# A hybrid decoder step on one core: the sample stage's first keys, last page and gate weights in another order

## What is computed

```python
def diff_attention(q, k, v, q_pos, k_pos, lam, lambda_init, subln):
    s = jnp.einsum("bqhmd,bkhmd->bhmqk", q, k) * (DH_D ** -0.5)
    s = jnp.where(k_pos[None, :] <= q_pos[:, None], s, -jnp.inf)
    p = jax.nn.softmax(s, axis=-1)
    a = p[:, :, 0] - lam * p[:, :, 1]
    o = jnp.einsum("bhqk,bkhv->bqhv", a, v)
    return rmsnorm(o, subln) * (1.0 - lambda_init)

# sample side: keys and values of the cache pages, then the own ones
k_all = jnp.concatenate([past_k, kd], axis=1)
v_all = jnp.concatenate([past_v, vd], axis=1)
o = diff_attention(qd, k_all, v_all, pos, k_pos, lam, lambda_init, subln)
...
y_b = o.reshape(B, T, D_D) @ w_proj_b
merged = jax.nn.sigmoid(g_a) * y_a + jax.nn.sigmoid(g_b) * y_b
x = x + merged @ w_out
x = x + 0.5 * swiglu(rmsnorm(x, ffn2_norm), ffn2_w_gate, ffn2_w_up, ffn2_w_down)
```

## Time and profile before

| | us |
|---|---|
| time, median of 3 runs (lowest to highest) | 1717.48 (1714.74 to 1723.19) |
| the profiled execution: time | 1720.7 |
| the profiled execution: span, first to last instruction | 1718.9 |
| PE busy in the span | 1664.8 (97%) |
| DVE, ACT busy | 765.6, 554.3 |

### The profile page before, as it was taken

How to read it: one execution, slowest core, us unless ns; L and a number is a source line. 1 busy time by engine, 2 the same in 40 slices (tenths; PEclk the granted TensorE clock), 3 DMA queues, 4 the chain that set the end, 5 groups by cost and what they waited for, 6 DMA issues and landing times.

```text
span 1718.9 us, 30602 instructions
## 1 busy us (share of the span) xinstructions
PE 1664.8 (97%) x12820; PEld 1571.5 (91%) x12820; DVE 765.6 (45%) x1150; ACT 554.3 (32%) x845; POOL 4.3 (0%) x20
## 2 busy tenths in 40 slices
PE   7999999999999999999999999989999999999996
PEld 7999999999988666999999977669999999999996
DVE  3333333333682433453336678664454333333332
ACT  5222222222332433442211257562234222222222
POOL 0000000000000000000000000000000000000000
PEclk8999999999999999999999999999999999999998
DMA  4322223322322740233333340553322332223231
GB/s 117 98 85 85 85 85 87 98 84 75 77 74 55 249 144 0 64 89 91 91 96 96 78 182 26 186 159 87 93 86 79 91 90 86 85 85 102 85 85 53
DMA packets 253837, 161.77 MB, mean 94 GB/s; under 512 B 8235, under 2 KB 246048, under 8 KB 253763
## 3 DMA queue, kind: packets, MB, share of 16 engines
q1 hardware_dynamic: 253616, 160.67, 32.2%
q10 hardware_dynamic: 146, 0.04, 0.0%
HBM read 143.14 MB, written 16.40 MB: 93 GB/s over the span
## 4 chain that ended last, share of the span: by engine, by line
PE 88%; ACT 3%; DVE 3%; DMA 2%; issue 1%; SPq 1%; ACTq 0%; DVEq 0%
PE ps L402 72%; PE ps L781 2%; PE ps L969 2%; PE ps L933 1%; PE ps L1257 1%; PE ps L1128 1%; PE ps L1185 1%; DMA Cb<-in_state_C 1%; PE ps L1018 1%; PE ps L1301 1%; PE ps L1113 1%; DVE small L2327 1%; PE ps L1182 1%; PE ps L1260 1%; DMA vecs<-in_subln 0%
## 5 line engine op out<-in xcount | busy, mean ns | idle before, releaser
L402 PE MATMUL ps<-xn_hi,w_hi 128*128 128x272 f32 (+1 forms) x2192 | 634.9, 290 | 4.7 <-DVE w_lo L374 2.6
L402 PE MATMUL ps<-xn_hi,w_lo 128*128 128x272 f32 (+1 forms) x2192 | 636.8, 290 | 0.0
L402 PE MATMUL ps<-xn_lo,w_hi 128*128 128x272 f32 (+1 forms) x2192 | 633.8, 289 | 0.0
L370 ACT ACTIVATE w_hi<-raw 128x1024 fp32r<-128x1024 f32 (+1 forms) x200 | 222.1, 1111 | 822.8 <-PE ps L402 818.2
L402 PEld LDWEIGHTS ps<-xn_hi,w_hi 128*128 128x128 f32 x2192 | 413.0, 188 | 6.3 <-DVE w_lo L374 3.1
L402 PEld LDWEIGHTS ps<-xn_hi,w_lo 128*128 128x128 f32 x2192 | 412.7, 188 | 0.0
L402 PEld LDWEIGHTS ps<-xn_lo,w_hi 128*128 128x128 f32 x2192 | 411.8, 188 | 0.0
L374 DVE TENSOR_TENSOR w_lo<-raw,w_hi 128x1024 fp32r<-128x1024 f32 (+1 forms) x200 | 257.5, 1288 | 214.8 <-ACT w_hi L370 214.2
L402 PE MATMUL ps<-h_lo,w_hi 128*128 128x280 f32 (+1 forms) x704 | 204.7, 291 | 0.0
L402 PE MATMUL ps<-h_hi,w_hi 128*128 128x280 f32 (+1 forms) x704 | 204.7, 291 | 0.0
L402 PE MATMUL ps<-h_hi,w_lo 128*128 128x280 f32 (+1 forms) x704 | 204.6, 291 | 0.0
(11 more groups left out here) (372 smaller groups left out, 2043.6 us busy)
## 6 DMA issues: line engine op xcount, KB each, us to landing
raw<-in_w_in SPq DMA_DIRECT2D x56, 512.0 KB, 3.9
raw<-in_ffn_w_gate SPq DMA_DIRECT2D x44, 512.0 KB, 3.8
raw<-in_ffn_w_up SPq DMA_DIRECT2D x44, 512.0 KB, 3.8
raw<-in_ffn_w_down SPq DMA_DIRECT2D x32, 704.0 KB, 4.5
Cb<-in_state_C SPq DMA_DIRECT2D x32, 256.0 KB, 4.0
out<-Cb SPq DMA_DIRECT2D x32, 256.0 KB, 3.1
pages<-in_cache_k SPq DMA_DIRECT2D x16, 512.0 KB, 4.5
pages<-in_cache_v SPq DMA_DIRECT2D x16, 512.0 KB, 4.7
```

The costliest lines, as they stand in the source:

```text
L370: act.activation(w_hi[s][:, 0:p.nk, :], raw[s][:, 0:p.nk, :], ACT.Copy).then_inc(hi_done[s], 1)
L402: mm = pe.matmul(ps[:, bank + half, 0:p.half], w[s][:, k, :], x[:, k0 + k, cols], start=first and k == 0 and a == 0, stop=last and k == p. ...
```

## The change

Six edits, all in and around the sample stage:

1. PE transposes the first three groups of the first page of keys in the last steps of "attend": behind `output(G - 3)`, ahead of `transposed(G - 1)` (G = 34 steps). They use banks that the scores had, after the last exponentials. The fourth group follows when PE's stage is over, and PE's `begin` is gone.
2. ACT and DVE copy the first keys ahead of their barrier. `head_square(0)`, `(1)` and DVE's `memset` of `AT3` come behind them. `head_sum(0)` moves from ahead of `score(0)` to behind it.
3. The last page of keys goes to slot 1 instead of slot 0.
4. SP loads the first gate panel to `raw[0]` when sequence 4's values are done, behind the last page in its queue; only the other panel waits for all keys.
5. ACT and DVE split that panel inside the loop at sequence 7: ACT ahead of the last exponentials, DVE ahead of the last mask and maximum.
6. PE runs four gate tiles ahead of `probabilities(7)`, two behind it, then `values(7)`, two and the second half's first, `back(1)`, three more, the sum, and the last four.

```diff
-        SLOTS = [i % 5 for i in range(13)] + [3, 4, 0]
+        SLOTS = [i % 5 for i in range(13)] + [3, 4, 1]
-        SUM_KEYS, SUM_SCORE = {0: 0, 1: 2, 2: 4, 3: 7}, {0: 1, 1: 3, 2: 5}
+        SUM_KEYS, SUM_SCORE = {1: 2, 2: 4, 3: 7}, {0: (0, 1), 1: (3,), 2: (5,)}
...
+            sp.wait_ge(sv_full, 5)
+            load(sp, p_b, 0, 0)
             sp.wait_ge(keys_full, 4 * NB)
-            stream_short(p_b)
+            load(sp, p_b, 0, 1)
+            for j in range(1, p_b.n):
+                load(sp, p_b, j, 0)
+                load(sp, p_b, j, 1)
...
                 if g >= 4:
                     output(g - 4)
+                if g == G + 1:
+                    pe.wait_ge(e_ready, G)
+                    keys(0, range(3))
             end(pe, pe_stage)
-            begin(pe, "sample")
...
             for b in range(NB):
-                keys(b)
+                keys(b, range(4) if b else range(3, 4))
...
-            probabilities(NB - 1)
             pe.wait_ge(evac[0], p_b.ev0)
             pe.wait_ge(lo_done[0], p_b.before + 1)
-            gate_part(0, range(2))
+            gate_part(0, range(4))
+            probabilities(NB - 1)
+            gate_part(0, range(4, 6))
             values(NB - 1)
-            gate_part(0, range(2, 5))
+            gate_part(0, range(6, DT))
+            gate_part(1, range(1))
             back(1)
-            gate_part(0, range(5, DT))
+            gate_part(1, range(1, 4))
             pe.wait_ge(osq_ready, HD + 1)
             pe.matmul(ps[:, 4, 0:HD * NS], ones[:, :], ofac[:, :, NP_:T], start=True, stop=True).then_inc(ring_full, 1)
-            gate_part(1, range(DT)).then_inc(mm_done[0], 1)
+            gate_part(1, range(4, DT)).then_inc(mm_done[0], 1)
...
-            begin(act, "sample")
+            act.wait_ge(tail_in, HD)
...
-            act.wait_ge(stored, 16 * (5 + 6))
-            head_square(0)
...
+                if b == 0:
+                    begin(act, "sample")
+                    act.wait_ge(stored, 16 * (5 + 6))
+                    head_square(0)
+                    head_square(1)
+                for h in (2,) if b == 0 else ():
+                    head_square(h)
+                if b == NB - 1:
+                    act.wait_ge(keys_full, 4 * NB)
+                    split_hi(act, p_b, 0, 0)
                 act.wait_ge(smax_ready, b + 1)
...
-            split_hi(act, p_b, 0, 0)
...
-            begin(v, "sample")
+            v.wait_ge(tail_in, HD)
+            for i in range(2):
+                v.tensor_copy(KT[0][i][:, :, PAST:PAST + NS], own_k[:, 4 * i:4 * i + 4, :])
...
+                if b == NB - 1:
+                    v.wait_ge(sv_full, NB - 2)
+                    split_lo(v, p_b, 0, 0)
                 v.wait_ge(ss_full, b + 1)
...
-            split_lo(v, p_b, 0, 0)
```

More of the change, by code:

```diff
@@ L1306, in output, with keys @@
                 mm.then_inc(o_full, 1)
+            def keys(b, groups=range(4)):
+                page_wait(pe, (0, b))
+                for n in range(4 * b + groups[0], 4 * b + groups[-1] + 1):
+                    g, q = n % 4 // 2, n % 2
+                    if n >= 3:
+                        m = n - 3
+                        if m % 2 == 0:
+                            pe.wait_ge(keys_act, m // 2 + 1)
+                        else:
+                            pe.wait_ge(keys_dve, m // 2 + 1)
+                    for i in range(4):
+                        hh = 4 * q + i
+                        mm = transpose(ps[:, n % 3, 128 * i:128 * i + 128],
+                                       pages[page_slot((0, b))][:, g, 128 * hh:128 * hh + 128], 128)
+                    mm.then_inc(keys_full, 1)
             for g in range(G + 4):
@@ L1413, in _ @@
                 score(b)
-                if b in SUM_SCORE:
-                    head_sum(SUM_SCORE[b])
+                for h in SUM_SCORE[b] if b in SUM_SCORE else ():
+                    head_sum(h)
                 if b >= 1:
@@ L1798, in _ @@
                     rows_out(0)
-                for h in (1, 2) if b == 0 else ():
+                if b == 0:
[4 more added lines that the diff above has]
+                for h in (2,) if b == 0 else ():
                     head_square(h)
+                if b == NB - 1:
+                    act.wait_ge(keys_full, 4 * NB)
+                    split_hi(act, p_b, 0, 0)
                 act.wait_ge(smax_ready, b + 1)
@@ L2401, in _ @@
                                   ps[:, (4 * b + 2 * g + 1) % 3, :].rearrange("p (h n) -> p h n", h=4)).then_inc(keys_dve, 1)
+                if b == 0:
+                    v.drain().then_inc(qh_ready, 1)
+                    begin(v, "sample")
+                    v.memset(AT3[:, :, :, :], 0.0)
+                    for i in range(2):
+                        v.tensor_copy(KT[1][i][:, :, PAST:PAST + NS], own_k[:, 4 * i:4 * i + 4, :])
                 if b in SUM_KEYS:
@@ L2412, in _ @@
                                 negate=True).then_inc(smax_ready, 1)
-                if b in SUM_SCORE:
-                    head_raw(SUM_SCORE[b])
+                for h in SUM_SCORE[b] if b in SUM_SCORE else ():
+                    head_raw(h)
                 v.wait_ge(sexp_ready, b + 1)
```

## The result

The changed kernel takes 1720.38 us (median of 20 runs, 1715.14 to 1727.16), the kernel before 1717.55 (20 runs). The ratio is 1.0018 [1.0010, 1.0027], which is 3.1 us slower [1.7, 4.6]. Run once more beside before (8 runs against 24), it was 1.0028 [1.0017, 1.0038], or 4.8 us. So it is slower by 0.2 to 0.3%, clear of noise and well under the 0.5% that the prediction set as its bound.

What follows compares the result with a forecast made beforehand. PE, busy 97% of the span, was taken as the bound, except in the sample stage's loop, where it waits on DVE and ACT. 0.15 + 0.76 = +0.9 us on the median 1717.48 gave 1718.4, range 1714.0 to 1723.5.

Steps and rivals of the forecast that it cites:

- The likeliest case: Whole change: 0.15 us at the stage's start plus 0.76 at the sum of squares, +0.9 us, 1718.4; chance 0.45.
- the clock's rival: PE's clock falls to half in the longer wait for the last page: +2.5 us, 1720.0; chance 0.25.
- second fall: The clock falls again in PE's new idle time behind the sum of squares: +1.6 us more, 1721.6 with both.
- The stage's start: Edits 1 and 2: last step of "attend" 0.69 us later, 0.54 won back; net 0.15 later, bounds -0.2 and +0.5.
- The last page: Last keys, waiting for `keys(6)`, come 2.80 us later (2.4 to 3.5); the score begins 1.65 later.
- the hidden page: Rival: the last page of keys comes within 1 us of before; -1.05 us, 1716.4; chance 0.2.
- the late gate panel: Rival: the gate panel, queued behind the late page, isn't in when ACT wants it; +1.3 us, 1718.8; chance 0.1.
- From the page to the scores: Sequence 7: 16 transposes and `probabilities(6)` without the old waits, so the score begins 2.85 us after the page.
- From the scores to the last probabilities: Sequence 7: DVE's low part delays the mask, cost 0.5 us; `probabilities(7)` moves from 1143.62 to 1145.76, 2.14 later.
- The tail: Behind `probabilities(7)`: DVE's norms set the sum of squares, 0.76 us later; PE then idles some 1.5 us.
- If the wait at the last probabilities is gone altogether: Sign of being wrong: PE's wait ahead of `probabilities(7)` vanishes; the gain would then be 1 to 3 us.
- The sum: Whole change: 0.15 at the stage's start plus 0.76 at the sum of squares makes +0.9 us.

Runs made afterwards that it cites:

- slot alone: The kernel before with edit 3 alone, the last page of keys in slot 1: 1.0012 of before, 2.1 us slower.
- the wait filled: The changed kernel with 13 matmuls of ones, adding no result, in PE's wait for the last page of keys: 1.0018 of before.
- end alone: The changed kernel with edits 1 and 2 undone: 1.0012 of before, 2.1 us slower by the middle value.
- start alone: The changed kernel with edits 3 to 6 undone: 0.9995 of before.
- the new waits filled: The changed kernel with matmuls of ones: 5 ahead of the first page's fourth group, 3 ahead of its scores, 13 ahead of the last page: 1.0005 of before.
- the fastest version: The changed kernel with sequence 4's values and sequence 6's keys in swapped slots and edits 1 and 2 undone: 0.9985 and 0.9991 of before.

## Why the prediction was right or wrong

The time lies in the range, and "within 0.5%" was right. The range was 9.5 us wide and held every case, so that says little. The likeliest case was not what happened: +0.9 us was forecast, 3.1 [1.7, 4.6] came (4.8 [2.9, 6.5] when run again), and the case that fits is the clock's rival, which had 0.25: +2.5 with a fall at the page. Its second fall, behind the sum of squares (+1.6), did not come: the granted clock is full there. Falls came at the start and in sequence 4 instead. By the steps:

**The stage's start**: right without the clock. The last output ends 0.51 us later (0.69 forecast) and the scores begin 0.07 earlier against the same mark (0.15 later forecast, -0.2 to +0.5). What failed is that I looked at the waits' ends only. The two new waits there, 1.34 and 0.87, are followed by a fall of the clock in four of the six profiles with this start left unfilled, 0.9 us by `score(1)` in the changed kernel, and in none of the seven with the old start. No case of mine had it.

**The last page**: right, and the step that decides. Release to use is 6.97 us (6.55 forecast), and PE's wait 3.61 (3.2 forecast). The slot alone loses 2.1 us, and swapping the slots of two earlier pages removes the loss. From issue to use it was 6.23 us. The Trainium skill's figures ("DMA: Bandwidth & Descriptors", section "Anatomy of one DMA"), given for another issuing path, 2.0 us and the bytes at 436 GB/s, make that an estimate of some 4.4 us; the trace sides with the row of before (5.8). Of the rivals, the hidden page did not come true, and the late gate panel neither: it cost ACT no wait.

**From the page to the scores**: 2.85 forecast. It is 2.90 with the wait filled and 5.27 in the changed kernel, at half clock. **From the scores to the last probabilities**: 4.79 forecast; 4.57 with the wait filled, 5.91 in the changed kernel. So the clock takes 2.4 + 1.3 = 3.7 us there by the profiles, where the rival had 1.6. The price was mis-sized: I put half clock on 3.5 us of PE's work at up to 1.6 more, as if it lasted for part of them. It lasted ten us and nearly doubled all of them: 16 transposes 3.68 against 2.00, the scores 2.15 against 1.18. For a shorter fall 1.6 would do: with the slot alone and the end alone, at half for 3.4 us, the way from the page to the scores is 4.45 and 4.17, 1.3 to 1.6 more.

**The tail**: right. From the last probabilities to the sum of squares 7.54 was forecast and 7.15 came; DVE's five norms set it, as said, and from there to "next" the time is the same in every kernel, with PE idle for 1.34 us (1.5 forecast). With a full clock the old tail takes 7.38 (start alone), so the gate tiles ahead save only 0.2 by themselves. Most of the 1.8 saved against before is the fall of the clock that before had there. "If the wait at the last probabilities is gone altogether" stood among the signs of being wrong, with a gain of 1 to 3 us. The wait went and no gain came: PE was at half clock in its place, behind a page that came 3 us late.

**The sum**: with the new waits filled the stretch is 0.4 us over the first profile of before, against +0.9 forecast, and the time 0.9 us over [-0.7, +2.6]. So the terms at full clock fit, as far as this can tell; against the second profile of before, 84.8, the stretch is 1.1 shorter. The step that failed is the weight between the cases: one row of a wait without a fall, at 1122, made me give the clock 0.25. That same wait of 1.77 us stands in six of the profiles, and behind it the clock fell in two. A wait of 2.8 us or more for the page, with PE idle, had a fall in it or just behind it in four of four. The rule of the Trainium skill ("TensorE: Matmul & The Clock Gate", section "What's actually happening"), that an idle array is throttled, gave 1720.0 and came nearest to the median of 1720.38. The trace agrees at the page, in all four profiles with the long wait. At the start it agrees in the changed kernel and not in the start alone.

What stays open: the profile's stretch does not rank the kernels by time at 1 to 2 us. Filling only the last wait shortened the stretch by 3.3 us and not the time, and the fastest version has a stretch longer than before's first. The part ahead of the stage alone differs by up to 7.6 us between two profiles. The mean granted clock over all runs goes with the times better (0.988 for the changed kernel, 0.991 for before and with all waits filled, 0.992 for the fastest). Over the 20 runs of the changed kernel, 0.001 more of it goes with 1.2 us less (correlation -0.93). As an estimate from that, the 0.0025 to 0.003 that the changed kernel's clock lies under before's go with some 3 us of its loss of 3.1 to 4.8, and 0.3 to 1.5 us are left for everything else, where the sum without the clock had 0.9. But where in those runs the clock fell isn't known. Nor did I find why it falls in sequences 4 and 5 of that version, or what decides whether it falls behind a wait of 1 to 2 us.

## What to carry to other kernels

Before a buffer is given to another transfer, write down what releases it: here the last page went from a buffer free with `values(4)` to one free with `keys(6)`, 2.8 us later, for a transfer that had no slack. Free the wanted buffer by an exchange among earlier, uncritical transfers instead. And price a new wait of the matmul engine twice, once for its length and once for the work behind it at half clock, as long as the fall may last. One wait of nearly the same length without a fall is no evidence that the next has none.

## What the runs showed of the hardware

Two executions of the changed kernel had the clock's falls at the same places, at the first scores, in sequence 4 and in the page's wait (stretch 88.6 and 88.7 us). I had taken them for chance. But the waits alone don't set them:

| PE's wait | at half in it or within 3 us behind it |
|---|---|
| 2.8 to 3.6 us for the last page, left unfilled | 4 profiles of 4 |
| 1.82 to 1.85 us ahead of the last probabilities | 3 of 4 |
| 1.34 and 0.87 us at the new start, left unfilled | 4 of 6 |
| 1.77 us ahead of sequence 5's last keys | 2 of 6 |

And before itself had one fall of 3.4 us in its first profile and two, of 3.4 and 6.8 us, in its second. One fall of the changed kernel kept the clock at half for ten us though PE was recorded busy in every window of it from 1134 on. Matmuls without use in the three new waits, 21 of them, made the changed kernel 2 to 4 us faster (1.0005 against 1.0028, or against 1.0018 the first time).
